# Seven half products: conditioning sums between the additions of the down products, weights of the second turn rounded on ScalarE

## What is computed

```
mod = silu(c) @ w_ada[l] + b_ada[l]              # and the same with c_ctx
...
x = layer_norm(ALPHA * x + g1 * y, ln1_g[l], ln1_b[l])
x = layer_norm(ALPHA * x + g2 * swiglu(x * (1 + sc2) + sh2, w_gu[l], w_down[l]), ...)

def swiglu(h, w_gu, w_down):                     # inner width 2816
    gate, up = split(h @ w_gu)
    return (silu(gate) * up) @ w_down
```

## Time and profile before

| | us |
|---|---|
| median of 3 runs | 3403.79 |
| lowest, highest | 3401.39, 3404.04 |
| the profiled execution, its own time | 3407.32 |
| its span in the trace | 3404.8 |

### The profile page before, as it was taken

One profiled execution on the slowest core, in us unless ns is written; L12 is line 12 of the kernel. 1 busy time (PEld: TensorE's weight loads), 2 busy tenths in 40 slices (PEclk: granted clock), 3 DMA queues, 4 the chain that ended last, 5 costly groups with the idle time before them and its releaser, 6 DMA issues. The chain is left out here.

```text
span 3404.8 us, 43534 instructions
## 1 busy us (share of the span) xinstructions
PE 3134.5 (92%) x16618; PEld 2659.2 (78%) x16618; DVE 2124.2 (62%) x3250; ACT 1163.9 (34%) x2235; POOL 1503.4 (44%) x1145
## 2 busy tenths in 40 slices
PE   4999989899999999978889899989899989999997
PEld 3798878788787888867678679878787768887886
DVE  8768977675784455455553746965786575554544
ACT  5267732452422222210001536742352322232013
POOL 0553222354354343444534554213354455455654
PEclk9999999999999999989889999999999989999999
DMA  9200051022132333443320200031022222225321
GB/s 341 71 1 1 1 178 31 21 94 74 38 132 85 110 103 119 140 167 106 114 96 32 100 13 2 1 106 46 18 81 87 89 79 93 75 77 177 98 88 50
DMA packets 99246, 283.79 MB, mean 83 GB/s; under 512 B 8416, under 2 KB 21856, under 8 KB 97632
## 3 DMA queue, kind: packets, MB, share of 16 engines
q1 hardware_dynamic: 92224, 256.90, 22.2%
q10 hardware_dynamic: 6816, 24.12, 1.8%
HBM read 226.72 MB, written 54.26 MB: 83 GB/s over the span
## 5 line engine op out<-in xcount | busy, mean ns | idle before, releaser
L4022 DVE SCALAR_TENSOR_TENSOR x_res<-ps,mod,x_res 128x512 f32<-128x512 f32 (+1 forms) x448 | 307.0, 688 | 258.0 <-PE ps L215 257.1
L213 PE MATMUL ps<-f_ahi,f_whi 128*128 128x512 f32 (+1 forms) x896 | 350.7, 391 | 67.4 <-DVE x_res L4022 61.0
L214 PE MATMUL ps<-f_alo,f_whi 128*128 128x512 f32 (+1 forms) x896 | 337.0, 376 | 0.0
L215 PE MATMUL ps<-f_ahi,f_wlo 128*128 128x512 f32 (+1 forms) x896 | 336.4, 375 | 0.0
L3398 POOL TENSOR_TENSOR h_a_lo<-f_wraw,h_a_hi 128x512 fp32r<-128x512 f32 x112 | 153.6, 1388 | 371.1 <-ACT h_a_hi L3393 371.1
L213 PEld LDWEIGHTS ps<-f_ahi,f_whi 128*128 128x128 f32 x896 | 177.8, 198 | 109.4 <-DVE x_res L4022 70.7
L214 PE MATMUL ps<-h_lo,h_a_hi 128*128 128x512 f32 (+1 forms) x640 | 224.0, 350 | 0.0
L213 PE MATMUL ps<-h_hi,whic 128*128 128x512 f32 (+1 forms) x544 | 198.9, 366 | 14.6 <-DVE wloc L465 14.6
L3774 POOL TENSOR_TENSOR f_alo<-f_gated,f_ahi 128x512 fp32r<-128x512 f32 (+1 forms) x85 | 117.2, 1398 | 205.8 <-ACT f_ahi L3963 205.8
L214 PEld LDWEIGHTS ps<-f_alo,f_whi 128*128 128x128 f32 x896 | 178.0, 199 | 31.1 <-issue 3.4
L215 PEld LDWEIGHTS ps<-f_ahi,f_wlo 128*128 128x128 f32 x896 | 177.4, 198 | 28.7
(11 more groups left out here) (395 smaller groups left out, 8929.5 us busy)
## 6 DMA issues: line engine op xcount, KB each, us to landing
f_wraw<-in_w_ffn SPq DMA_DIRECT2D x130, 512.0 KB, 4.5
ada_w<-in_w_ada SPq DMA_DIRECT2D x56, 512.0 KB, 6.2
h_hi_f<-in_w_ada SPq DMA_DIRECT2D x56, 512.0 KB, 4.0
o_wraw<-in_w_out SPq DMA_DIRECT2D x28, 512.0 KB, 3.6
wrawc<-in_w_in SPq DMA_DIRECT2D x24, 512.0 KB, 4.1
act_spill<-f_gated SPq DMA_DIRECT2D x18, 640.0 KB, 3.4
f_gated<-act_spill SPq DMA_DIRECT2D x17, 640.0 KB, 6.3
x_spill<-x_res ACTq DMA_DIRECT2D x16, 640.0 KB, 6.0
```

Source lines behind the costliest of these rows:

```text
L213: pe.matmul(out, w_hi, h_hi, start=first, stop=False)
L214: pe.matmul(out, w_hi, h_lo, start=False, stop=False)
L215: return pe.matmul(out, w_lo, h_hi, start=False, stop=last)
L4022: dve.scalar_tensor_tensor(out=x, in0=pl.bank(down_bank(i) + d % 2, tn), scalar=pl.mod[:, G2 + n, who:who + 1], in1=x, op0=ALU.mult, op1=A ...
```

## The change

Three edits, with no instruction of the conditioning sums, of TensorE or of SP added or removed.

First, in layer 0's down turns the sums stand inside `add`: after the groups 3, 9, 14 and 19 of the turn. Turns with two sums use the first two places, those with three the first three. SP's queue is the same. Second, `split_second` leaves the rounding of turn 1's four weight blocks to ScalarE (`round_second`, both layers) and GpSimd keeps the subtraction. Third, in the last pair `round_down(0)` stands right behind ScalarE's first copy (both layers), ahead of its wait for `c11`.

```
             act.activation(self.a[:, :], self.bank(p, 0), ACT.Copy).then_inc(self.a_in, 1)
+        if ahead is not None:
+            ahead()
         self.wait_result(act, "c11", p)
...
             def split_second(j):
-                pool.wait_ge(loaded[(j + 1) % 2], 48 + 16 * (j // 2 + j % 2))
-                if j in (1, 2):
-                    pool.wait_ge(down_full, n_down + 1)
-                else:
-                    pool.wait_ge(gu_full[1], 4 + {0: 1, 3: 2}[j])
-                split(6 + j, (j + 1) % 2, slot[j])
+                place = slot[j]
+                pool.wait_ge(turn_rounded, j + 1)
+                pool.tensor_tensor(w.lo[place][:, :], w.raw[(j + 1) % 2][:, :], raw(w.hi[place][:, :]),
+                                   ALU.subtract).then_inc(ready, 1)
...
+            def round_second(j):
+                act.wait_ge(loaded[(j + 1) % 2], 48 + 16 * (j // 2 + j % 2))
+                if j in (1, 2):
+                    act.wait_ge(down_full, n_down + 1)
+                else:
+                    act.wait_ge(gu_full[1], 4 + {0: 1, 3: 2}[j])
+                act.activation(w.hi[slot[j]][:, :], w.raw[(j + 1) % 2][:, :], ACT.Copy).then_inc(turn_rounded, 1)
+
+            round_second(0)
             seven.spill(act, norm.split[1], down_taken, n_down - KT + 3)
+            round_second(1)
+            round_second(2)
             seven.round_t(act, 1)
             silu(1, 0, chunks)
+            round_second(3)
...
-            def first_of_down():
-
+            def ahead_of_down():
                 seven.wait_made(act, "m7", pairs - 1)
                 round_down(0)
+
+            def first_of_down():
+
                 seven.wait_used(act, "a12", pairs - 1)
                 round_down(1)
...
                     if after is not None:
                         after.after_add(dve, c, n)
+                    if items and d in (3, 9, 14, 19):
+                        ada.product(dve, items.pop(0))
...
-                    add(i, c)
-                    if items:
-                        ada.product(dve, items.pop(0))
-                for n in items:
-                    ada.product(dve, n)
+                    add(i, c, items=items)
```

More of the change, by code:

```diff
@@ L3481, in tensor, with scalar @@
         product("m3", "s4", *plain(1, 512, 512), self.bank(p, 2), True)
-    def scalar(self, act, p, between=None):
+    def scalar(self, act, p, between=None, ahead=None):
         more = p + 1 < self.COUNT
@@ L3611, in feed_forward @@
     down_rounded, down_ready = sem("down_rounded"), sem("down_ready")
-    first_down_rounded = sem("first_down_rounded")
+    first_down_rounded, turn_rounded = sem("first_down_rounded"), sem("turn_rounded")
     raw_act_in = [sem(f"raw_act_in{f}") for f in range(2)]
@@ L3713, in _, with split @@
             one = pl.small[:, 2:3].broadcast_to([P, D])
-            def split(number, par, place):
+            def split(number, par, place, others=0):
                 hi, lo = w.hi[place][:, :], w.lo[place][:, :]
                 pool.tensor_tensor(hi, w.raw[par][:, :], one, ALU.mult).then_inc(rounded, 1)
-                pool.wait_ge(rounded, number)
+                pool.wait_ge(rounded, number - others)
                 pool.tensor_tensor(lo, w.raw[par][:, :], raw(hi), ALU.subtract).then_inc(ready, 1)
@@ L3747, in split_last @@
                     pool.wait_ge(gu_full[1], LAST_TURN * 4 + {3: 2, 4: 3, 5: 4}[j])
-                split(LAST_READY + j, (j + 1) % 2, slot[j])
+                split(LAST_READY + j, (j + 1) % 2, slot[j], 4)
             def split_down(i, f):
@@ L3975, in _ @@
             for p in range(pairs):
-                between = None
+                between = ahead = None
                 if p == pairs - 1:
-                    between = first_of_down
+                    between, ahead = first_of_down, ahead_of_down
                 elif p == 0 and ada is not None:
                     between = lambda: ada.silu(act, 0)
-                seven.scalar(act, p, between)
+                seven.scalar(act, p, between, ahead)
             for i in range(1, end):
@@ L4011, in gate, with add @@
                     dve.tensor_tensor(g, g, pl.bank(3 + c, tn), ALU.mult).then_inc(u_taken[c], 1)
-            def add(i, c, after=None):
+            def add(i, c, after=None, items=None):
                 t0, tn = CHUNKS[c] if after is None else after.spans[c]
```

## The result

| | us |
|---|---|
| before, median of 10 runs beside it | 3402.38 (3399.39 to 3404.93) |
| after, median of 10 runs | 3410.86 (3399.58 to 3414.37) |
| after / before | 1.0023, 95% interval 1.0013 to 1.0033 |
| the profiled execution of after | 3411.28 (span 3409.3) |

The change made the kernel 7.8 us slower (4.4 to 11.2). I had forecast +2.1. The profiled execution of before took 3407.32, more than any of the ten other runs, so the two spans show only +4.5. I therefore compare stage by stage.

The account below looks back on a forecast made before the run. TensorE, busy 92% of the span, was taken as the bound, so only its pauses and lower-clock stretches could be won. +9.2 - 4.5 - 2.6 = +2.1 us took the median from 3403.8 to 3405.9, written 3406; range 3397 to 3416.

Parts of the forecast that it names:

- First edit, forecast +9.2: Layer 0's down turns: turns 1 to 8 lengthen behind the first sum's late load, turn 9 shortens by 7.4; sum +9.2 us.
- I take 2.7: Layer 0's down turns: 2.7 us per turn for the lower clock behind a pause, with 0.3 us stops for later sums.
- 38.9: Layer 0: length in us of a down turn in the new order, from landing, sum, groups and lower clock.
- My slower rival: Layer 0: each turn's first sum still runs beside a GpSimd instruction, 2.76 us instead of 1.15, +12.9, so 3419; slower 27%.
- the landing at 11.2: Layer 0's down turns: the first sum's weight block still lands 11.2 us after the turn's start, as SP's queue is untouched.
- my faster rival: Layer 0: the landing comes earlier, at 9.5 us, or sums don't stop TensorE in turns 6 to 8; -11.9, so 3394; 14%.
- Second edit, forecast -4.5 in layer 1 and 0 in layer 0: Turn 1: ScalarE's rounding shortens VectorE's chain of input sums by 4.5 us in layer 1; layer 0 gains nothing.
- The replay by turns: Layer 1, turn 1: VectorE and GpSimd instructions taking turns; the eighth input sum ends at 2758.3 instead of 2762.8.
- Third edit, forecast -2.6: Start of layer 1's down turns: one subtraction leaves TensorE's chain, its 5.4 us pause becomes 2.8, -2.6 us; layer 0 gains 0.
- the possible 1.6 for the clock: Start of layer 1's down turns: up to 1.6 us more gained if the pause gets too short to lower the clock.
- Its smaller form: Layer 0, within slower's 27%: landing at 12.0 us instead of 11.2 gives +5.6 more, 3411.5.
- the bound that I wrote down for it: First edit, layer 0: the clock's cost at 3.4 us in eight turns gives +15 instead of +9.2.

Follow-up runs that it names:

- the last one: The changed kernel with each turn's first sum loaded ahead of two stored-value loads, no sums in turn 1, places 8, 13, 18 and 22: 3320.25 us.
- the one with late places and moved counts: The changed kernel with sums behind groups 11, 15, 19 and 22, and turn 1's three sums moved to turns 2, 3 and 4: 3334.59 us.

## Why the prediction was right or wrong

The forecast was 3406.0, no change; the kernel became 0.23% slower (0.13 to 0.33), 3410.9, inside the range of 3397 to 3416. By my own bound of 0.2% this is just on the slower side, and the interval takes in the bound. The direction of each edit was right; the size of the whole was not, +2.1 us against +7.8 and +10.5 in the two measurements. Most steps held. One term of the first edit was mis-sized, since it hides two cases and a second sum beside GpSimd.

**First edit, forecast +9.2, about +17.** It measures +20.4 (15.6 to 24.8) alone against before; +15 to +18 as after's two ratios over that of the second and third edit (1.0023 and 1.0031 over 0.9978); and +17.2 as the down turns' mean in three traces with it (354.3) less that of four without (337.1: before 338.3, and 335.5, 337.1 and 337.4 in the other three). Of the 8 us that I was short:

- The step that failed is "I take 2.7" for the stretch at the lower clock with the stops for later sums. It was drawn from three rows that ranged from 1.5 to 3.4, and I took a value between. With each turn's own landing and my 25.05 for the sum and the groups taken off, turns 3 and 4 leave 1.85 when short and 4.35 when long. The turn has two lengths, and 38.9 is neither. Over turns 2 to 8 of the three traces with the edit the term is 3.8 on average, 7.5 us too little in seven turns. Landings 0.3 us earlier on average than I had them gave 2.2 of that back; with rounding, the seven turns are 5.6 us longer than my 273.5. In the first trace of after they sum to 273.5, to the tenth what I had worked out, and that is luck: only three of them were long, and the landings came 0.6 us early. In the two other traces five were long: 280.4 and 283.5.
- The trace of before already had both sizes. Behind TensorE's pauses in turns 2 to 9 the granted clock stayed at half for 5.3, 5.4, 6.0, 3.4, 5.2, 6.1, 6.2 and 3.2 us, six long and two short. My three rows were those of turns 4, 5 and 9: one of the six long ones and both short ones. TensorE's stretch at half clock behind the pause, turns 4 and 5 of before (columns as above):

```profile
1584.50:1590.60 6.10, 6.05 (x14) 4.79 (x15) 1.93 (x3) 0.00 (x0) 1.55 (x1) 0.50 0.74 258
1621.35:1624.70 3.35, 3.35 (x8) 2.67 (x9) 0.99 (x2) 0.00 (x0) 3.27 (x3) 0.50 0.49 157
```

These stand behind pauses of 5 to 6 us, and the two sizes are the same behind the longer pauses of after. Behind the pauses of turns 2 to 8 the lower clock cost 18.8 us in before and 15.0 to 17.5 in the three traces with the first edit. So it is not a dearer clock that makes the edit slow.

- What I missed inside this term is the second sum. I argued that the first one would be undisturbed, since GpSimd's split waits for the chunk behind it, and it is (1.22 or 1.23 everywhere). But that split then starts 5.3 us behind the end of the first sum (1518.65 against 1513.36 in turn 2), and in a turn whose clock is slow to come back the second sum arrives when the subtraction has already begun. I had written "the next one waits for the chunk behind the sum" and not asked what stands behind that chunk. The Trainium skill (page "SBUF — State Buffer", section "SBUF: two separate sides") says that whichever of the two starts first keeps the shared port pair for its whole instruction, while the other waits. The trace agrees, in both orders: 2.45 us for a sum of 1.22 in turn 2, and 3.26 for a subtraction of 2.40 in turn 3. My slower rival acted, then, one sum later than I placed it.
- Turn 1 took 3.3 us more on average than in before, not 2.1. In after its block landed 2.2 us later than before (1471.33 against 1469.15 in the earlier trace rows).
- Before's own down turns, 338.3 us in the trace that I had, were 1.2 longer than the mean of the four.

Confirmed as written: the undisturbed first sum, turn 9 at 28.3 exactly, and nothing at a turn's end; in turns 2 to 4 also the landing at 11.2 (10.9 to 11.2), the wait of 7 to 8 us and TensorE's pause of 8 (7.6 to 8.0). Turn 5's landing was 12.05. In turns 6 to 8, which have four sums, it was 9.9 to 10.4 in the first trace of after, with waits of 6.0 to 6.5 and pauses of 6.7 to 7.2, and 10.3 to 11.6 in the two others. That is, in part, the earlier landing of my faster rival, and I don't know what moves it.

**Second edit, forecast -4.5 in layer 1 and 0 in layer 0: -4.35 and 0.** The replay by turns held in its order: the fourth and fifth sum alone (2.29 each), the sixth behind a subtraction (4.50), the seventh behind T1's rest, which is twice as wide (6.69), the eighth over 29.1 us after the start where I had 29.0. In layer 0 VectorE's wait for TensorE ahead of T4's rest grew from 4.03 to 11.71, as an earlier chain only waits longer.

**Third edit, forecast -2.6: -2.75.** One subtraction left the path, as said; no part of the possible 1.6 for the clock is needed, a term for which I had shown no row.

**The rivals.** The slower one came true in its price, by the second sum and the clock in place of the first sum. Its smaller form, 3411.5 by a landing at 12.0, gave the right time for a wrong reason: the landings were 9.9 to 11.2 but for turn 5. 27% for slower was too little: of the three rows that priced the clock, the dearest alone led to +15, the bound that I wrote down for it. I gave that bound no case of its own, though it was the size that six of eight turns of before had.

**What stays open.** The first edit alone measured 20.4 (15.6 to 24.8), with the others 15 to 18. The intervals overlap, and each trace has its own count of long turns, so I can't say that the edits act on one another. Nor is it known what decides how long the lower clock stays behind the same pause, or why the landings of turns 6 to 8 differ by up to 1.4 us between traces.

## What to carry to other kernels

Where an engine waits for a transfer, the time of the landing is what counts: moving the consumer ahead of other work doesn't bring the transfer sooner, and leaves less work done when everyone stops. Ask first what the load stands behind in its queue; here one load issued ahead of two waiting ones gave 57 us, and the same sums placed behind the landing gave 65.

When a cost read from the trace comes in two sizes, count in that trace how often each size occurs and keep both as cases: here the long one stood in six turns of eight, and I had read one of them. A value between is right only when the counts happen to balance.

## What the runs showed of the hardware

Behind a pause of 8.00 us TensorE worked about 6 us at the lower clock (1.2 GHz of 2.4) in one turn, and behind one of 7.64 us about 3 in the next, with the same instructions ahead of it. Which turns were which changed from one execution to another of the same program. The kernel before shows both sizes too, behind pauses of 5 to 6 us. The changed kernel's 19 runs in two measurements spread over 18.7 us (3399.58 to 3418.28). Whether that comes from the long and short turns isn't shown: of the versions without such pauses, the five runs of the last one spread over 6.4, but the five of the one with late places and moved counts over 13.2.

A VectorE sum with two SBUF inputs takes 1.22 us alone. Where it starts behind a GpSimd instruction (a rounding, a subtraction, the rest of inner values) it takes 1.3 to 3.4 in the traces here, the more the more of that instruction is left. Where it starts ahead of one, GpSimd's instruction is the longer one (3.26 us for 2.40). By the estimate above a second sum beside a split costs its turn 1.0 us more than one alone.
